# Cached index keys turned by single-pass transpositions, and sample dots over 64 rows

## The reference, cut to what matters

```
dots  = einsum('bqhd,bkd->bqhk', iq, ik_all) * IDX_DIM ** -0.5     # 16 x 8 rows, 272 keys, over 64
score = einsum('bqh,bqhk->bqk', iw, relu(dots))                    # weighed over the 8 heads
_, idx = top_k(score, n_top)
```

## Time and profile before

| | us |
|---|---|
| median of 3 runs | 1501.37 |
| lowest and highest | 1498.94, 1502.94 |
| the profiled execution: span from first to last instruction (of its time no more is shown) | 1504.3 |
| TensorE busy | 1449.8 (96%) |
| VectorE busy | 885.3 (59%) |
| ScalarE busy | 576.7 (38%) |
| GpSimd busy | 388.6 (26%) |

### The profile page before, as it was taken

The page is one execution under the profiler, slowest core; times in us unless marked ns, Lnnn a source line. Parts: engine busy times, 40 slices in busy tenths (PEclk is TensorE's granted clock), DMA queues, the critical chain, the costliest instruction groups (busy, mean ns, idle before and its releaser), DMA issues. The chain is left out here.

```text
span 1504.3 us, 28580 instructions
## 1 busy us (share of the span) xinstructions
PE 1449.8 (96%) x11446; PEld 1352.6 (90%) x11450; DVE 885.3 (59%) x1644; ACT 576.7 (38%) x1141; POOL 388.6 (26%) x352
## 2 busy tenths in 40 slices
PE   5999999999999999999998989999999999999997
PEld 4899999999999999999896767799999999999997
DVE  5546674575467451677567656563657448744764
ACT  5433331442334343544335424532544124422444
POOL 1603322340341341431001120112722034403400
PEclk9999999999999999999999979999999999999999
DMA  9534543545453233232115030233113312330231
GB/s 341 167 115 127 167 142 113 158 144 161 127 168 101 71 69 90 71 70 71 29 28 136 2 89 17 72 106 84 57 43 98 99 53 82 92 113 29 85 99 70
DMA packets 213784, 148.76 MB, mean 99 GB/s; under 512 B 18075, under 2 KB 190396, under 8 KB 213656
## 3 DMA queue, kind: packets, MB, share of 16 engines
q1 hardware_dynamic: 210488, 137.54, 31.1%
q0 software_dynamic: 3168, 9.42, 2.3%
HBM read 139.99 MB, written 6.95 MB: 98 GB/s over the span
## 5 line engine op out<-in xcount | busy, mean ns | idle before, releaser
L1167 PE MATMUL pair<-b_hi,w_hi 128*128 128x320 f32 x720 | 224.3, 312 | 0.0
L1167 PE MATMUL pair<-b_hi,w_lo 128*128 128x320 f32 x720 | 222.5, 309 | 0.0
L1167 PE MATMUL pair<-b_lo,w_hi 128*128 128x320 f32 x720 | 222.4, 309 | 0.0
L1285 PE MATMUL pair<-act_hi,w_hi 128*128 128x320 f32 x656 | 150.7, 311 | 0.0
L1285 PE MATMUL pair<-act_hi,w_lo 128*128 128x320 f32 x656 | 149.5, 309 | 0.0
L1285 PE MATMUL pair<-act_lo,w_hi 128*128 128x320 f32 x656 | 149.4, 309 | 0.0
L1167 PEld LDWEIGHTS pair<-b_hi,w_hi 128*128 128x128 f32 x720 | 135.1, 188 | 14.3 <-DVE w_lo L666 8.4
L548 DVE SCALAR_TENSOR_TENSOR x_t<-pair,gate,x_t 128x320 f32<-128x320 f32 x120 | 52.5, 480 | 157.0 <-PE pair L1285 132.0
L660 ACT ACTIVATE w_hi<-sums_a 128x512 fp32r<-128x512 f32 x72 | 45.1, 627 | 251.9 <-POOL sums_a L694 131.7
L1049 DVE TENSOR_TENSOR uvw<-pair,uvw 128x320 f32<-128x320 f32 (+1 forms) x126 | 67.6, 537 | 122.9 <-PE pair L1167 122.9
L1167 PEld LDWEIGHTS pair<-b_lo,w_hi 128*128 128x128 f32 x720 | 135.2, 188 | 0.0
(11 more groups left out here) (478 smaller groups left out, 3239.1 us busy)
## 6 DMA issues: line engine op xcount, KB each, us to landing
w_mod_raw<-w_mod SPq DMA_DIRECT2D x28, 1024.0 KB, 5.8
w_raw<-ffn_w_gate SPq DMA_DIRECT2D x40, 512.0 KB, 4.1
raw_more<-ffn_w_up SPq DMA_DIRECT2D x40, 512.0 KB, 3.8
w_raw<-w_in SPq DMA_DIRECT2D x24, 512.0 KB, 3.8
w_raw<-ffn_w_down SPq DMA_DIRECT2D x16, 384.0 KB, 3.3
raw_more<-ffn_w_down SPq DMA_DIRECT2D x16, 384.0 KB, 3.2
w_mod_a<-w_mod SPq DMA_DIRECT2D x4, 1024.0 KB, 10.7
w_mod_b<-w_mod SPq DMA_DIRECT2D x4, 1024.0 KB, 11.2
```

The lines of the kernel that those rows point to most:

```text
L1167: mm = pe.matmul(job_bank(j, BANK_OF[part]), w[:, at, kk], mv[:, kk, s], start=(kk == 0 and v == 0 and part in FIRST_OF_BANK), stop=(kk == ...
L1285: mm = pe.matmul(pair[part % 2][:, b, 0:HALF], w[:, slot, k], mv[:, k, b * HALF:(b + 1) * HALF], start=(k == 0 and v == 0), stop=(k == n - ...
```

## The change

The turning takes two transpositions for each sample in place of four matmuls, and fills partitions 0 to 63 alone. ScalarE copies these 64 partitions. `iq_z` has all its 128 columns on rows 0 to 63: for odd heads VectorE copies from partitions 64 to 127 down to 0 to 63. The dots contract over these 64 rows. The memset of `iq_z` is gone.

```diff
-                        act.activation(ik_tb[:, b % 2], bank[0][:, 0:PAST], ACT.Copy).then_inc(S["ikb"], 1)
+                        act.activation(ik_tb[0:AD, b % 2], bank[0][0:AD, 0:PAST], ACT.Copy).then_inc(S["ikb"], 1)
...
-            link(dve.memset(iq_z[:], 0.0))
...
-                            ins = dve.tensor_copy(iq_z[rows, :, at:at + TB], smp(iq_t[rows, j_, SEQ:]))
+                            ins = dve.tensor_copy(iq_z[0:AD, :, at:at + TB], smp(iq_t[rows, j_, SEQ:]))
...
                         for k in range(2):
-                            for par in range(2):
-                                mm = pe.matmul(bank[0][AD * par:AD * (par + 1), k * P:(k + 1) * P], ik_raw[:, b, k], ident,
-                                               start=True, stop=True)
+                            mm = pe.transpose(bank[0][0:AD, k * P:(k + 1) * P], ik_raw[:, b, k], ident)
                         mm.then_inc(S["ikb_turned"], 1)
                         if b >= 1:
                             weigh(b - 1)
                         pe.wait_ge(S["ikb"], b + 1)
-                        pe.matmul(bank[1][:, 0:PAST], iq_z[:, b], ik_tb[:, b % 2], start=True, stop=True)
-                        pe.matmul(bank[1][:, PAST:LS], iq_z[:, b], ik_t[:, SEQ + b * TB:SEQ + (b + 1) * TB],
+                        pe.matmul(bank[1][:, 0:PAST], iq_z[0:AD, b], ik_tb[0:AD, b % 2], start=True, stop=True)
+                        pe.matmul(bank[1][:, PAST:LS], iq_z[0:AD, b], ik_t[0:AD, SEQ + b * TB:SEQ + (b + 1) * TB],
                                   start=True, stop=True).then_inc(S["sdots"], 1)
```

## The result

| | before | changed |
|---|---|---|
| median of 6 runs on the same chips, us | 1504.57 | 1511.87 |
| lowest, highest | 1498.94, 1507.45 | 1510.93, 1515.39 |
| profiled span | 1504.3 | 1513.6 |
| ratio, with 95% interval | | 1.0059 (1.004 to 1.0078) |

Slower by 0.6%, outside my range of 1498.3 to 1505.2. The side that I gave 7% came out.

The account below looks back on a forecast made before the run. TensorE, at work for 1449.8 of 1504.3 us, was taken to bound the kernel. Visits of +0.06, twice +0.18 and +0.07 summed to +0.49 us, carried over to the median of 1501.37: 1501.9, range 1498.3 to 1505.2.

Parts of the forecast that it names:

- The side that I gave 7%: Whole kernel: the chance of 0.07 for slower, against 0.06 for faster and 0.87 for the same within 0.3%.
- Only they can change: Four short visits after projection units, where cached index keys are turned, multiplied and weighed: some 17 us, 1.1% of the span.
- rival 4: Attention, as from 872 to 892 us: one more stretch at clock 0.50, up to 9.5 us slower, 1511; chance 0.05.
- The sum of +0.49: All four visits: gains from turning sooner and costs of changes of form, together 0.49 us slower.
- Passes get no shorter: Dots over 64 rows: passes take as long as before, but a change of form drains TensorE, 0.10 us each.
- Turning gives nothing in first halves and 0.03 in second ones: Visits' halves: turning sooner only lengthens TensorE's wait in first halves; weighing comes 0.03 us sooner in second ones.
- Change of form, +0.18 in the second and third visit, +0.07 in the last: Weighing to dots costs 0.10 us, dots to `L2628` 0.11 (not in the last visit), each less 0.03 gained.
- First visit, +0.06: First visit: 0.19 us gained by turning sooner, against 0.10, 0.04 and 0.11 for changes of form.
- the 0.19: First visit: `ik_tb` waits for the turned keys and could start at 703.84 instead of 704.03, 0.19 us gained once.
- The memset, "0": Start of the mixer: removing VectorE's memset of `iq_z`, 0.91 us, changes the time by 0; 1 us faster if none were hidden.
- no change of form is paid: Visits: no cost for going between 128 and 64 rows; 0.28 us faster, 1501.1; chance 0.22.
- the stream decides: TensorE in the visits: each pass removed counts, 1.8 to 2.6 us faster, about 1499; chance 0.09.

Follow-up runs that it names:

- k64_m_second: t2_k64_ms with the second sample of each visit turned by matmuls (four passes), the first still by transpositions; ratio 1.0031 to the kernel before.
- t2_k64_late: t2_k64_ms with spare 128-column matmuls in second halves, behind the second turning and the last dots; output not the reference's; ratio 1.0011 to the kernel before.
- t2_k80: t2_k128 with dots that contract over 80 rows, 16 of them zeros; ratio 1.0031 to the kernel before.
- t2_k128: Kernel before with keys turned by two transpositions a sample, dots still over 128 rows (rows 64 to 127 zeroed); ratio 1.0009.
- before_poolms: Kernel before with the memset of iq_z done by GpSimd, nothing else of the edit; ratio 0.9995.
- before_att: Kernel before with 45 spare matmuls in TensorE's waits in the attention alone; 1495.30 us against 1502.26, ratio 0.9951.
- t2_k64_ms: Changed kernel with the memset of iq_z back in VectorE's program, nothing else; ratio 1.0063 to the kernel before.
- t2_k64_fill: t2_k64_ms with two spare 128-column matmuls in each first half, in TensorE's wait for ik_tb; ratio 1.0058 to the kernel before.
- after: The changed kernel itself, with the whole edit, against the kernel before; 1511.87 us, ratio 1.0059.
- m8_k64: Kernel before, keys still turned by eight matmul passes, with dots over 64 rows and no memset; ratio 1.0032.
- m4_k64: Changed kernel with its two transpositions replaced by two matmuls of two passes each, to the same 64 partitions; ratio 1.0037 to the kernel before.

## Why the prediction was wrong

- **The step that failed** is "Only they can change": the sum took the clock of 1.00 around the visits as given and had no term for it, and in rival 4 the condition was "It decides once the new waits come near that 1.63". The clock was a rival at 5% and its place was the attention. It fell at the end of the visits themselves, with no wait there above 0.81 us, and cost 6.3 us of the 7.2. What the runs put in its place: work in the second halves that costs little or nothing by the timeline was what held the clock, for it held again when such work was put back (0.86 to 0.94 in k64_m_second, to 1.00 in t2_k64_late). Which of its properties the clock goes by (time at work, passes, rows) stays open.
- **Luck.** Rival 4's 1511 is near the 1511.87 measured. That is chance: it stood for one more stretch of 20 us in the attention, not for three short ones behind the visits, and from a median before that was 3.2 us lower.
- **The sum of +0.49** measured +0.89 (1.25 less 0.36). The second, third and last visit came to +0.14, +0.14 and +0.07, the first to +0.54.
- **"Passes get no shorter", so fewer rows are free but for drains.** As timing right. Whether the number of rows counts for the clock isn't shown. t2_k80 was slower than t2_k128 (1.0031 against 1.0009, with intervals that overlap; median clock 0.979 against 0.985). But their visits are equally long and both have 0.97 over them; their profiled executions part elsewhere, in the attention (t2_k128, then t2_k80):

```profile
796.00:906.00 110.00, 95.80 (x1549) 0.92 0.27 71
```
```profile
796.00:906.00 110.00, 97.46 (x1466) 0.88 0.28 72
```

- **Turning gives nothing in first halves and 0.03 in second ones:** right. From the second turning to the weighing took 0.59 us before and takes 0.55 now. That t2_k128's visits are 4.03 long against 4.07 doesn't show it by itself: they begin 0.09 sooner, and as dots and transpositions have one form there, 0.08 of the step between them goes too (0.14 for 0.22), which the prediction didn't price.
- **Change of form, +0.18 in the second and third visit, +0.07 in the last:** measured +0.23 and +0.16, each less the 0.09 by which the turning starts sooner behind the projection, so +0.14 and +0.07. That 0.09 also shows that narrow transpositions don't change the form, as taken from `L2905`.
- **First visit, +0.06:** mis-sized. I read the second half as hanging on the relu. In the kernel before, the relu and `v_beta` ended at the same time (705.73, 705.72), and `v_beta` doesn't move with the turning, so the 0.19 weren't gained. With the memset kept it measured +0.29, without it +0.63, each less 0.09 again.
- **The memset, "0":** no cost on TensorE at 542 us, right, but taking an instruction out of VectorE's program cost some 0.3 us 160 us later. before_poolms, where GpSimd does the memset and ScalarE waits for it, shows it without the rest of the edit: first visit 3.97 instead of 3.71. In the whole time it can't be seen (0.9995).
- **Two rivals:** "no change of form is paid" fell by the 0.66 and 0.22 of the timeline; "the stream decides" by t2_k128, with 48 passes fewer and no gain. The price in rival 4 (up to 9.5 us for a stretch of 20) holds as the upper bound that it was meant to be: before_att, without any such stretch from 796 to 906 us, where 13.2 us had been lost to the clock, is 7.0 us faster.

Open: how much of the rest (1.0011 for t2_k64_late, of which 0.1% is its own spare work) is clock. Whether the rows or the zeros in them matter wasn't tried. Why VectorE's instruction starts late when its program is one instruction shorter isn't known either; where the instructions lie when they are fetched was my theory, and before_poolms agrees with it without telling it from others. One slip in the description of the kernel: `IN_UNITS` has 30 units, not 32. And most kernels have one profiled execution and 4 to 10 timed ones, so differences of 0.2% between them are at the edge of what can be told.

## What to carry to other kernels

Where TensorE holds its full clock through a passage of short, uneven work, passes that look free can be what holds it, as here: before taking work out, ask what the granted clock does in the sparser passages of the same trace. Test the halves of an edit both alone and together, for neither half alone showed the whole of this loss. And where TensorE waits a microsecond for other engines and the clock falls behind it, a few spare matmuls into a bank about to be overwritten are worth trying; here 45 of them gave 0.5%. Judge them by the times of many executions, since such a stretch can also be missing from one profile by itself.

## What the runs showed of the hardware

- Longer visits can be the faster ones: t2_k64_ms (four visits of 4.00, 4.30, 4.30, 5.42) and t2_k64_fill (the same lengths) had a granted clock of 0.86 and 0.89 over the visits, t2_k64_late, with three of them 0.55 us longer, 1.00.
- A change of form between matmuls that follow each other without a wait cost 0.08 to 0.10 us at each place: weighing to dots 0.66 us with 64 rows, 0.56 with 128; from the last dots to the one-column matmuls 0.22 and 0.14; from dots to turning 0.22, and 0.14 in t2_k128, where both have the form of 128.
- One VectorE instruction fewer can delay a later one: in all four kernels without the memset in VectorE's program (after, m8_k64, m4_k64, before_poolms) the two instructions shown above started 0.40 us apart in the first visit, put down to issue, and 0.07 or 0.08 in the others.
